# Gate rows turned in four pieces, one key copied earlier, small products of the mLSTM units joined

## The reference

```python
mq, mk, mv, mo, mg, aq, ak, av, bg = jnp.split(h @ w_in, idx, axis=-1)
...
b = jnp.cumsum(fc, axis=-1)
dmat = jnp.where(lower, b[..., :, None] - b[..., None, :] + ic[..., None, :], -jnp.inf)
inter = b + m[..., None]
m_t = jnp.maximum(inter, jnp.max(dmat, axis=-1))
w_inter = jnp.exp(inter - m_t)
s = jnp.einsum("bhtd,bhsd->bhts", qc, kc) * jnp.exp(dmat - m_t[..., None])
num = (w_inter[..., None] * jnp.einsum("bhtd,bhde->bhte", qc, C)
       + jnp.einsum("bhts,bhse->bhte", s, vc))
den = w_inter * jnp.einsum("bhtd,bhd->bht", qc, n) + jnp.sum(s, axis=-1)
h = num / jnp.maximum(jnp.abs(den), jnp.exp(-m_t))[..., None]
```

## Time and profile before

| | |
|---|---|
| median of 3 runs | 1716.31 us (1714.97 to 1716.84) |
| span of the profiled execution | 1715.9 us |
| TensorE busy | 1695.8 us (99%) |
| VectorE busy | 1046.0 us (61%) |
| ScalarE busy | 688.1 us (40%) |
| read from and written to HBM | 170.67 and 16.54 MB, 109 GB/s |

### The profile page before, as it was taken

The page is one execution under the profiler, slowest core; times in us unless marked ns, Lnnn a source line. Parts: engine busy times, 40 slices in busy tenths (PEclk is TensorE's granted clock), DMA queues, the critical chain, the costliest instruction groups (busy, mean ns, idle before and its releaser), DMA issues.

```text
span 1715.9 us, 28055 instructions
## 1 busy us (share of the span) xinstructions
PE 1695.8 (99%) x11327; PEld 1564.3 (91%) x11327; DVE 1046.0 (61%) x1777; ACT 688.1 (40%) x1254; POOL 0.2 (0%) x4
## 2 busy tenths in 40 slices
PE   8999999999999999999999999999999999999998
PEld 6999899989979989999999888889989988998997
DVE  5756465666465314555536877775646844982885
ACT  6322222212364322344355554553474433541453
POOL 0000000000000000000000000000000000000000
PEclk9999999999999999999999999999999999999999
DMA  9435443433314224332342311101521221222233
GB/s 387 174 135 217 139 159 135 156 139 123 90 59 160 74 62 104 85 97 80 86 150 81 113 53 41 41 27 64 209 75 73 81 93 61 97 89 86 74 99 148
DMA packets 58651, 189.50 MB, mean 110 GB/s; under 512 B 7672, under 2 KB 16680, under 8 KB 56744
## 3 DMA queue, kind: packets, MB, share of 16 engines
q1 hardware_dynamic: 58536, 187.89, 32.7%
HBM read 170.67 MB, written 16.54 MB: 109 GB/s over the span
## 4 chain that ended last, share of the span: by engine, by line
PE 91%; DVE 3%; ACT 3%; issue 1%; DMA 0%; DVEq 0%; SPq 0%; ACTq 0%
PE psum L709 13%; PE psum L710 12%; PE psum L711 12%; PE psum L812 4%; PE psum L691 4%; PE psum L693 4%; PE psum L814 4%; PE psum L692 4%; PE psum L813 4%; PE psum L1233 2%; PE psum L1215 2%; PE psum L782 2%; PE psum L783 2%; PE psum L781 2%; PE psum L1193 2%; PE psum L1118 1%
## 5 line engine op out<-in xcount | busy, mean ns | idle before, releaser
L1866 DVE TENSOR_TENSOR wlo<-raw,whi 128x1024 fp32r<-128x1024 f32 x148 | 181.2, 1224 | 370.4 <-ACT whi L1327 370.3
L1327 ACT CAST whi<-raw 128x1024 fp32r<-128x1024 f32 x148 | 155.1, 1048 | 325.0 <-PE psum L814 140.7
L709 PE MATMUL psum<-h_hi,whi 128*128 128x320 f32 x720 | 223.8, 311 | 0.0
L711 PE MATMUL psum<-h_hi,wlo 128*128 128x320 f32 x720 | 222.5, 309 | 0.0
L710 PE MATMUL psum<-h_lo,whi 128*128 128x320 f32 x720 | 222.4, 309 | 0.0
L709 PE MATMUL psum<-g_hi,whi 128*128 128x320 f32 x656 | 209.4, 319 | 0.2 <-ACT gate L1684 0.2
L711 PE MATMUL psum<-g_hi,wlo 128*128 128x320 f32 x656 | 202.7, 309 | 0.0
L710 PE MATMUL psum<-g_lo,whi 128*128 128x320 f32 x656 | 202.6, 309 | 0.0
L709 PEld LDWEIGHTS psum<-h_hi,whi 128*128 128x128 f32 x720 | 135.1, 188 | 4.6 <-issue 4.5
L710 PEld LDWEIGHTS psum<-h_lo,whi 128*128 128x128 f32 x720 | 135.2, 188 | 0.0
L711 PEld LDWEIGHTS psum<-h_hi,wlo 128*128 128x128 f32 x720 | 135.1, 188 | 0.0
(11 more groups left out here) (442 smaller groups left out, 3733.1 us busy)
## 6 DMA issues: line engine op xcount, KB each, us to landing
raw<-in_w_ffn_in SPq DMA_DIRECT2D x88, 512.0 KB, 3.6
raw<-in_w_mix SPq DMA_DIRECT2D x77, 512.0 KB, 4.1
raw<-in_w_ffn_out SPq DMA_DIRECT2D x44, 512.0 KB, 3.5
mw<-in_w_mod SPq DMA_DIRECT2D x28, 768.0 KB, 5.1
mw<-in_w_mod SPq DMA_DIRECT2D x8, 1024.0 KB, 16.1
gate<-gate_keep SPq DMA_DIRECT2D x24, 320.0 KB, 4.9
mw<-in_w_mod SPq DMA_DIRECT2D x14, 512.0 KB, 4.5
gate_keep<-gate SPq DMA_DIRECT2D x20, 320.0 KB, 4.7
```

The costliest lines, as they stand in the source:

```text
L709: mm(out, wh[:, k, :], hi[:, k, cols], start=(k == 0), stop=False)
L711: last = mm(out, wl[:, k, :], hi[:, k, cols], start=False, stop=(k == nk - 1))
L1327: copy((to or whi[t.slot])[:, :, :], raw[t.raw][:, :, :]).then_inc(w_hi, 1)
L1866: tt(lo[:, :, :], raw[t.raw][:, :, :], hi[:, :, :].bitcast(F32), ALU.subtract).then_inc(raw_free, 1)
```

## The change

The turned gate rows are issued by `mv_tile`: a fourth after each half of the values tiles 1 and 2 (three groups of transposes, then the small products). VectorE copies the turned key 2 before the split of its step, no longer after it. In TensorE's loop over the units, the second half of a projection tile comes directly behind the first, and `spread_m`, `front_of`, `nums_of` and `turn_hm` follow in one block. ScalarE's and SyncE's code is the same.

```diff
--- before.py
+++ after.py
@@ -1011,6 +1011,8 @@
                             if v % 4 == 0 and o == 0:
                                 bank_free(c)
                             last = passes(c, o)
+                        if v in (1, 2):
+                            turn_gates(2 * (v - 1) + o)
                     last.then_inc(tile_done, 1)
                 else:
                     for n, c in enumerate(MV_LAST[f]):
@@ -1029,15 +1031,20 @@
                     last = tp(flat(2 + jb % 2)[:, c * P:(c + 1) * P], src[:, c * P:(c + 1) * P], ident)
                 last.then_inc(tr_done, 1)
 
-            def turn_gates():
-                pe.wait_ge(row_a, 6)
-                pe.wait_ge(row_d, ROW_END)
-                for q, src in enumerate((gi, gf, gm)):
+            def turn_gates(q):
+                if q == 0:
+                    pe.wait_ge(tr_ev, 3)
+                    pe.wait_ge(row_a, 6)
+                    pe.wait_ge(row_d, ROW_END)
+                if q < 3:
+                    src = (gi, gf, gm)[q]
                     for c in range(NT):
                         for d in range(2):
                             o = ((q * NT + c) * 2 + d) * H
                             last = tp(psum[:, 5, o:o + H], src[:, d, c * P:(c + 1) * P], ident[0:H, 0:H])
-                last.then_inc(tok_t, 1)
+                    if q == 2:
+                        last.then_inc(tok_t, 1)
+                    return
                 pe.wait_ge(sel_in, 3)
                 for j in range(4):
                     last = mm(psum[:, 5, (24 + j) * 2 * NT:(25 + j) * 2 * NT], sel2[0:H, j, :].bitcast(F32),
@@ -1054,9 +1061,6 @@
                     turn(0)
                 if L_MK + 2 <= l <= L_MV:
                     turn(l - L_MK - 1)
-                if l == L_MK + 6:
-                    pe.wait_ge(tr_ev, 3)
-                    turn_gates()
             half_gemm(0)
 
 
@@ -1135,9 +1139,9 @@
             for n in range(UNITS):
                 if n + 1 < UNITS:
                     half_gemm(10 + 2 * n)
+                    half_gemm(11 + 2 * n)
                     spread_m(n + 1)
                     front_of(n + 1)
-                    half_gemm(11 + 2 * n)
                 else:
                     half_gemm(2 * (L_AV - L_MO))
                 nums_of(n)
@@ -2455,6 +2459,8 @@
                 if l == 1:
                     select_rows()
                 elif l > 3:
+                    if l == L_MK + 3:
+                        take_turned(2)
                     split(Tile(T_MIX + l + 2))
                 if l == 4:
                     dve.wait_ge(tile_done, Tile(T_MIX + 3).n + 3)
@@ -2471,7 +2477,7 @@
                     tt(t_pair[32:H2, :, :], t1[:, :, :], t_pair[0:H, :, :].bitcast(F32), ALU.subtract).then_inc(t_in, 1)
                 if l == L_MK + 2:
                     take_turned(0)
-                if L_MK + 2 <= l <= L_MV:
+                if l == L_MK + 2 or l == L_MV:
                     take_turned(l - L_MK - 1)
                 if l == L_MK + 6:
                     take_gates()
```

## The result

The changed kernel takes 1723.25 us (median of 5 runs, 1722.70 to 1724.18), beside 1716.31 us for the kernel before in the same session. The medians are 6.9 us apart; the ratio on record is 1.0046, 95% interval 1.0035 to 1.0056, which is 6.0 to 9.6 us. The forecast was 1722. The profiled execution took 1723.12 us, its span 1721.3 us, 5.4 more than the span before; the sum had said 5.8.

The account below looks back on a forecast made before the run. TensorE was taken to bound the kernel, its records covering 99% of the span. Units' loss 9.2 less gate rows 2.7 and key 0.7 gave +5.8: 1721.7 us by the span, 1722 us for the runs, range 1717.5 to 1728.

Parts of the forecast that it names:

- the sum had said 5.8: Whole kernel: units' loss of 9.2 less gains of 2.7 (gate rows) and 0.7 (key) makes it 5.8 us slower.
- The loss of 9.2: Joined units: nineteen take 195.5 us beside 186.30, a loss of 9.2, bounds 6.9 to 12.6.
- The chain of 3.32: Between two tiles: spread, four VectorE products, exponential, eviction and return to TensorE take 3.32 us, bounds 3.2 to 3.5.
- its softest link: In the units' chain: hand-over from TensorE to VectorE ahead of the four products, taken as short, 0.04 us.
- a unit of 10.29: Joined unit: 6.97 us of tile products plus 3.32 us of chain, beside 9.01 in the first token tile and 9.95 later.
- What joining would save: Units: one entry and exit of small products less, 0.1 to 0.2 us each, 2 to 4 us in all without waits.
- the rival "the eviction stays hidden": Units: ScalarE's eviction or the chain ends early enough, joining saves 2 to 4 us, kernel about 1710 us; chance 0.08.
- The key: Values stage: VectorE copying turned key 2 before the split ends a TensorE wait, gain 0.7 us, bounds 0.5 to 0.7.
- "Gain 2.7": Gate rows in four pieces: 6.2 us removed, 3.5 added, gain 2.7 us, bounds 2.0 to 3.1 if the clock stays up.
- the 6.2 us that they replace: Gate rows: the undivided block of transposes and small products with its half-pace after-effects on TensorE costs 6.2 us.
- this offset: Whole kernel: runs' median 1716.31 us taken as 0.4 us above the profiled span of 1715.9, added at the end.
- The falling clock in the joined units: Rival: waits drop TensorE's clock, about 3 us a fall; 1734 us in four units, about 1779 in all 19; chance 0.10.

Follow-up runs that it names:

- key alone: Only the turned key copied ahead of the split, on the kernel before: 1714.92 us, ratio 1.0000.
- joined units alone: Only the units' products joined, on the kernel before, with gate rows and key as before: 1724.55 us, ratio 1.0047.
- the kernel with the new order: The whole change, with ScalarE evicting the projection tile ahead of the next unit's exponential: 1713.45 us, ratio 0.9989.
- the dose test: The whole change, with ScalarE casting the next weight tile ahead of the eviction in the units, making it 0.94 us later: 1746.03 us, ratio 1.0175.
- block with the new order: Kernel before with key copied earlier, units joined, ScalarE's eviction ahead of the exponential, gate rows in one block: 1714.08 us, ratio 0.9994.
- two pieces (two kernels): Changed kernel with gate rows in two pieces: units as before the change, 1714.27 us; units joined with ScalarE's eviction ahead of the exponential, 1713.80 us.
- four kernels with units at full clock: Gate rows in four pieces: change without joined units 1714.80 us; eviction ahead of exponential, joined 1713.45, not joined 1715.27; gate rows alone 1715.35.

## Why the prediction was right

**The units: right in mechanism and size.** The loss of 9.2 measured 8.8 over the same 19 tiles (186.30 to 195.12). The chain of 3.32 measured 3.31, its softest link, TensorE to VectorE, 0.05 (815.65 to 815.70) where 0.04 was taken; a unit of 10.29 measured 10.27. That the cause is the order in ScalarE's queue is shown from both sides: taking the eviction forward removes the loss, delaying it by 0.94 lengthens each unit by 0.94.

**What joining would save: wrong.** The prediction priced one entry and exit less at 0.1 to 0.2 us a unit, 2 to 4 us, if nothing waited. With nothing waiting it was 0.0 per unit: nums had been entered at pace all along, and what the exit cost is paid between the scores and nums instead. It didn't touch the forecast, since the chain covered it, but the rival "the eviction stays hidden" was some 2 us too good. The price had been read at the spread and was then used for another kind of product.

**The key: right**, 0.69 of 0.7 in the stage, too little for the time to tell.

**The gate rows: the failed step.** "Gain 2.7" was 2.2 in profiles (2.9 in the stage of the changed kernel, less 0.7 for the key) and none in the time (ratio 1.0001, an interval that leaves at most 1.4 us). Two things were mis-sized. The pieces cost 3 x 0.93 + 1.20 = 4.0, not 3.5: from ten transposes to the next big product are 0.72 (599.17 to 599.89) where 0.62 was taken, and the small products at full clock take 0.99 (603.51 to 604.50) where 0.8 was taken. And the 6.2 us that they replace were taken as a property of the code, from one execution. They are one of three cases: of the six profiles of a block, two have a long fall (before, key alone), one a short one (joined units alone) and three none. The undivided block adds 3.0 us with no fall (600.55 to 604.05, less two products), 6.2 with the long one, and 4.6 with the short one (the stage of 76.20 is 1.6 above 74.64). Against 4.0 the pieces lose 0.9 (by the stages, 75.63 less 74.64 is 1.0), gain 0.6 or gain 2.2. What decides which case comes, no run shows.

How often each comes can be estimated from the mean granted clock, which is given for 184 of these executions. The profiles with the block show what it goes with: 0.997 with the long fall, 0.998 with the short one, 0.999 or 1.000 with none. The measure is rough, because the mean also holds the end of the span, which differs between profiles. The last windows of the kernel with the new order, then of the kernel before, profiled again:

```profile
1700.00:1710.00 10.00, 5.45 (x25) 4.17 (x23) 6.60 (x8) 2.50 (x9) 0.00 (x0) 0.88 0.21 83
1710.00:1711.50 1.50, 0.00 (x0) 0.00 (x0) 0.00 (x0) 0.00 (x0) 0.00 (x0) 0.50 0.39 149
```

```profile
1710.00:1712.30 2.30, 0.00 (x0) 0.00 (x0) 0.00 (x0) 0.00 (x0) 0.00 (x0) 0.84 0.61 228
```

That is 2.0 and 0.4 us of clock lost there; the short fall of the joined units loses 1.7 (604 to 608 us). So a single execution can stand one column off. Counts of executions, from all sessions:

| gate rows | 0.999 to 1.000 | 0.998 | 0.997 |
|---|---|---|---|
| one block: the kernel before | 47 | 35 | 4 |
| one block: joined units, key alone, block with the new order | 13 | 8 | 6 |
| two pieces (two kernels) | 17 | 5 | 0 |
| four pieces (after, and four kernels with units at full clock) | 49 | 0 | 0 |

So the mechanism held as far as profiles show it: in none of six (the five kernels of the last line and the dose test) did the clock fall behind four pieces. That none of 49 executions is under 0.999 agrees, without excluding a short fall in some. But the block keeps the clock too, in three profiles of six and, by the counts, in 47 of 86 executions of before. Its mean price by these counts is (47 x 3.0 + 35 x 4.6 + 4 x 6.2) / 86 = 3.8, an estimate that takes the mean clock for the fall; the times of before rise with it, though less evenly (means of 1714.8, 1715.6 and 1718.2). The pieces' 4.0 are level with that, as the time says.

So the sum came out near, 5.8 for the 5.4 of the spans, and the runs differ by 7 because the profiled execution of before was a slow one, with the long fall. Its span of 1715.9 was put 0.4 us below the runs' median. In all other profiles the time of an execution is 1.8 us over its span (1723.12 to 1721.3, 1714.04 to 1712.3), which puts that execution at 1717.7, 1.4 above the median. The errors of the pieces, of the block and of this offset partly cancelled. That is luck: what was taken off for the long fall stood in the execution from which the sum started, and by the counts in 10 of 113 executions with a block.

**The falling clock in the joined units** didn't come with the change. It came with the dose test, so a chance of one in ten wasn't out of place. The Trainium skill ("TensorE: Matmul & The Clock Gate", section on HAM oscillation) says that pauses between bursts of products drop the clock. The dose test agrees at the waits of 2.19 us (695.12) and 1.98 us (719.08) and not at that of 1.98 us between them (707.87); the block shows that a stretch without a pause, of small products alone, can do the same.

The version that measured best is the changed one with ScalarE's two lines swapped: 0.9989 of the kernel before, some 10 us better than the change as it was. Its interval (0.9980 to 0.9998) just excludes no change, but the three versions with that order (0.9989, 0.9991, 0.9994) can't be told apart, and the other two intervals don't exclude it.

## What to carry to other kernels

When the order of one engine is changed, read the queues of the others for the same stretch: an order that did no harm as long as the spread came half a tile before the eviction puts a chain of five steps between two tiles when the spread comes after the tile. A gain that rests on the clock of one profile needs a second profile of the same code before it enters the sum. And the price of a switch between kinds of products is known only for the pair of kinds at which it was read.

## What the runs showed of the hardware

- Behind the same sparse block of 2.9 us (30 transposes of 8 columns, four products of ten columns) the granted clock stayed at 1.00 (before, profiled again), fell to 0.50 until about 607.5 us (joined units alone) or until 611 us (before), from one execution to the next. In the two-piece kernels, 1.9 us of transposes alone let it fall in one profile and not in another.
- In the dose test, a wait of 1.98 us with 2.3 us of small products ahead of it let the clock fall at one place (719.08 us) and not 11 us earlier (707.87); waits of 1.03 and 1.25 us with the same products did not, in the profile of the change.
- The price of small products hangs on what stands before them: four products for nums took 0.53 us behind a tile and 0.65 behind the scores.
